# Feed-forward input products of a split-fp32 block stack: three products of 256 columns, or one of 512 and one of 256

## What is computed

```
def rms_norm(x, g):
    y = x * rsqrt(mean(x * x, axis=-1) + 1e-6)
    return y * g

def swiglu(x, w_in, w_out):            # w_in 1024 x 5632, w_out 2816 x 1024
    g, u = split(x @ w_in, 2)
    return (silu(g) * u) @ w_out

for i in range(2):
    h = h + 0.5 * swiglu(rms_norm(h, ffn1_norm[i]), ffn1_w_in[i], ffn1_w_out[i])
    h = h + mixer_i(rms_norm(h, mix_norm[i]))      # recurrent, then spatial gating
    h = h + 0.5 * swiglu(rms_norm(h, ffn2_norm[i]), ffn2_w_in[i], ffn2_w_out[i])
```

## Time and profile before

| | |
|---|---|
| median of 3 runs | 1516.98 us (1516.81 to 1517.42) |
| profiled execution, its time | 1516.46 us |
| its span | 1514.7 us |
| TensorE products in flight | 1473.3 us, 97% |
| VectorE busy | 1051.7 us, 69% |
| ScalarE busy | 770.3 us, 51% |
| GpSimd busy | 293.9 us, 19% |
| DMA | 239.15 MB, mean 158 GB/s |

### The profile page before, as it was taken

The page is one execution under the profiler, slowest core; times in us unless marked ns, Lnnn a source line. Parts: engine busy times, 40 slices in busy tenths (PEclk is TensorE's granted clock), DMA queues, the critical chain, the costliest instruction groups (busy, mean ns, idle before and its releaser), DMA issues.

```text
span 1514.7 us, 31434 instructions
## 1 busy us (share of the span) xinstructions
PE 1473.3 (97%) x11919; PEld 1454.8 (96%) x11919; DVE 1051.7 (69%) x2005; ACT 770.3 (51%) x1296; POOL 293.9 (19%) x361
## 2 busy tenths in 40 slices
PE   7999999899999999999999999999999999999998
PEld 7999999899999999999999999999999999999898
DVE  6666578766655666557766665898768769976883
ACT  5455448554544545445454544536744453575442
POOL 4111113211102111024221113422240125121000
PEclk9999999999999999999999999999999999999999
DMA  6666754465555556555465555543343554434333
GB/s 203 186 186 201 222 171 132 149 192 180 183 177 184 183 181 191 172 192 168 140 194 174 186 163 172 167 112 108 97 115 101 167 141 140 116 95 125 112 119 119
DMA packets 245276, 239.15 MB, mean 158 GB/s; under 512 B 15160, under 2 KB 244392, under 8 KB 245176
## 3 DMA queue, kind: packets, MB, share of 16 engines
q1 hardware_dynamic: 245176, 237.78, 51.5%
HBM read 236.70 MB, written 1.05 MB: 157 GB/s over the span
## 4 chain that ended last, share of the span: by engine, by line
PE 84%; DVE 11%; ACT 2%; issue 2%; POOL 1%; DMA 0%; SPq 0%; DVEq 0%; ACTq 0%; POOLq 0%
PE bank L565 25%; PE bank L567 25%; PE bank L566 25%; DVE w_lo L1561 3%; DVE work L2023 1%; PE bank L893 1%; PE bank L851 1%; PE bank L833 1%; DVE work L1711 1%; PE bank L762 1%; PE bank L816 1%; PE bank L899 1%; PE bank L909 1%; DVE work L1594 1%; PE bank L832 0%
## 5 line engine op out<-in xcount | busy, mean ns | idle before, releaser
L1561 DVE TENSOR_TENSOR w_lo<-raw,w_hi 128x1024 fp32r<-128x1024 f32 (+1 forms) x456 | 558.3, 1234 | 296.5 <-ACT w_hi L982 296.1
L565 PE MATMUL bank<-x_hi,w_hi 128*128 128x256 f32 (+1 forms) x2480 | 717.1, 289 | 1.7 <-DVE w_lo L1561 1.6
L567 PE MATMUL bank<-x_hi,w_lo 128*128 128x256 f32 (+1 forms) x2480 | 705.7, 285 | 0.0
L566 PE MATMUL bank<-x_lo,w_hi 128*128 128x256 f32 (+1 forms) x2480 | 705.0, 284 | 0.0
L982 ACT CAST w_hi<-raw 128x1024 fp32r<-128x1024 f32 (+1 forms) x456 | 464.4, 1028 | 237.4 <-PE bank L567 227.1
L565 PEld LDWEIGHTS bank<-x_hi,w_hi 128*128 128x128 f32 x2480 | 474.3, 191 | 3.5 <-issue 2.0
L566 PEld LDWEIGHTS bank<-x_lo,w_hi 128*128 128x128 f32 x2480 | 474.4, 191 | 0.9
L567 PEld LDWEIGHTS bank<-x_hi,w_lo 128*128 128x128 f32 x2480 | 474.1, 191 | 0.0
L565 PE MATMUL bank<-y_hi,w_hi 128*128 128x256 f32 (+1 forms) x1088 | 310.6, 285 | 8.3 <-DVE y_lo L1572 8.3
L567 PE MATMUL bank<-y_hi,w_lo 128*128 128x256 f32 (+1 forms) x1088 | 309.7, 285 | 0.0
L566 PE MATMUL bank<-y_lo,w_hi 128*128 128x256 f32 (+1 forms) x1088 | 309.6, 285 | 0.0
(11 more groups left out here) (296 smaller groups left out, 1204.1 us busy)
## 6 DMA issues: line engine op xcount, KB each, us to landing
raw<-in_ffn_w_in_dram SPq DMA_DIRECT2D x176, 512.0 KB, 3.6
raw<-in_w_in_dram SPq DMA_DIRECT2D x100, 512.0 KB, 3.6
raw<-in_ffn_w_out_dram SPq DMA_DIRECT2D x64, 512.0 KB, 4.3
raw<-in_w_out_dram SPq DMA_DIRECT2D x32, 512.0 KB, 3.5
raw<-in_ffn_w_out_dram SPq DMA_DIRECT2D x32, 384.0 KB, 3.1
raw<-in_rec_w_in_dram SPq DMA_DIRECT2D x16, 512.0 KB, 3.5
raw<-in_sg_w_in_dram SPq DMA_DIRECT2D x16, 512.0 KB, 3.6
raw<-in_rec_w_out_dram SPq DMA_DIRECT2D x8, 512.0 KB, 3.5
```

What stands on the lines that cost most here:

```text
L565: mm(acc, wh, xh, start=first and j == 0, stop=False)
L566: mm(acc, wh, xl, start=False, stop=False)
L567: i_ = mm(acc, wl, xh, start=False, stop=last and j == n - 1)
L1561: TT(w_lo[:, s, 0:n, :], raw[:, s, 0:n, :], w_hi[:, s, 0:n, :].bitcast(fp32), SUB).then_inc(lo_made, 1)
```

## The change

x_hi and x_lo become the two halves of one tensor x_both, y_hi and y_lo those of y_both. In the in stages (both=True) a k takes two products: upper weights with both halves of the activations, 512 columns, a whole bank (columns 0 to 255 upper, 256 to 511 lower), and lower weights with the upper activations, into columns 256 to 511. A tile is then the sum of its bank's two halves. ScalarE copies the second half to SBUF (low_half, into ffn_b, which lies in the tensor pre, not in use there), VectorE adds the first half out of the bank, and multiplies the sum in SBUF; this second operation marks the bank as read. All other stages have three products of one k as before.

```diff
         w_hi = sb("w_hi", [P, RING, KU, CU], fp32r)
...
-        x_hi = sb("x_hi", [P, NC8 * L], fp32r)
-        x_lo = sb("x_lo", [P, NC8 * L], fp32r)
...
+        x_both = sb("x_both", [P, 2, NC8 * L], fp32r)
+        y_both = sb("y_both", [P, 2, NF * SEQ], fp32r)
+        x_hi, x_lo = x_both[:, 0, :], x_both[:, 1, :]
+        y_hi, y_lo = y_both[:, 0, :], y_both[:, 1, :]
...
+        ffn_b = pre[:, :, 3:3 + SEQ]
...
+                        if both:
+                            mm(bank[T % 4][:, 0:2 * N], wh, xs[:, :, a:b], start=first and j == 0, stop=False)
+                            i_ = mm(bank[T % 4][:, N:2 * N], wl, xs[:, 0, a:b], start=False, stop=last and j == n - 1)
                         else:
...
-                        mm(acc, wh, xh, start=first and j == 0, stop=False)
-                        mm(acc, wh, xl, start=False, stop=False)
-                        i_ = mm(acc, wl, xh, start=False, stop=last and j == n - 1)
+                            mm(acc, wh, xs[:, 0, a:b], start=first and j == 0, stop=False)
+                            mm(acc, wh, xs[:, 1, a:b], start=False, stop=False)
+                            i_ = mm(acc, wl, xs[:, 0, a:b], start=False, stop=last and j == n - 1)
...
+            def low_half(pr, m, i):
+
+                if m == 0:
+                    act.wait_ge(first_done, FIRSTS[pr] + 1 + 2 * i)
+                else:
+                    act.wait_ge(unit_done, units_of(pr)[-1][0] + 1 + 4 * i)
+                nc.scalar.copy(ffn_b[:, m, :], bank[(2 * pr + m) % 4][:, SEQ:2 * SEQ]).then_inc(low_copied, 1)
+
             def gate_turn(pb, ub, i, first=None):
...
                 for m in range(2):
+                    low_half(pb, m, i)
+                for m in range(2):
                     act.wait_ge(tile_read, 2 * pb + m + 1 + o4)
                     activation(ffn_s[:, m, :], ffn_t[:, m, :], ACT.Silu).then_inc(silu_done, 1)
                 for U in (ub + 2, ub + 3):
                     split_w(U + LEAD, o)
+                for m in range(2):
+                    low_half(pb + 1, m, i)
...
                 for m in range(2):
-                    scaled(pb, m, ffn_t[:, m, :], SEQ, META, o)
+                    dve.wait_ge(low_copied, 44 * f + m + 1 + 4 * i)
+                    TT(ffn_t[:, m, :], tile(pb, m, SEQ), ffn_b[:, m, :], ADD).then_inc(halves_added, 1)
+                for m in range(2):
+                    dve.wait_ge(halves_added, 44 * f + m + 1 + 4 * i)
+                    TT(ffn_t[:, m, :], ffn_t[:, m, :], rstd[:, META:L], MUL).then_inc(tile_read, 1)
                 for U in (ub + 2, ub + 3):
                     split_w(U + LEAD, o)
                 for m in range(2):
-                    wait_tile(pb + 1, m, o)
+                    dve.wait_ge(low_copied, 44 * f + m + 3 + 4 * i)
+                    TT(ffn_h[:, m, :], tile(pb + 1, m, SEQ), ffn_b[:, m, :], ADD).then_inc(halves_added, 1)
+                for m in range(2):
+                    dve.wait_ge(halves_added, 44 * f + m + 3 + 4 * i)
                     dve.wait_ge(gate_scaled, 22 * f + m + 1 + 2 * i)
-                    TT(ffn_h[:, m, :], tile(pb + 1, m, SEQ), ffn_r[:, m, :], MUL).then_inc(tile_read, 1)
+                    TT(ffn_h[:, m, :], ffn_h[:, m, :], ffn_r[:, m, :], MUL).then_inc(tile_read, 1)
```

More of the change, by code:

```diff
@@ L206, in build_stack @@
         h = sb("h", [P, NC8, L])
-        x_hi = sb("x_hi", [P, NC8 * L], fp32r)
-        x_lo = sb("x_lo", [P, NC8 * L], fp32r)
-        y_hi = sb("y_hi", [P, NF * SEQ], fp32r)
-        y_lo = sb("y_lo", [P, NF * SEQ], fp32r)
+        x_both = sb("x_both", [P, 2, NC8 * L], fp32r)
+        y_both = sb("y_both", [P, 2, NF * SEQ], fp32r)
+        x_hi, x_lo = x_both[:, 0, :], x_both[:, 1, :]
+        y_hi, y_lo = y_both[:, 0, :], y_both[:, 1, :]
         con = sb("con", [P, CONST_ALL])
@@ L322, in build_stack @@
         act_new = sem("act_new")
-        silu_done, gate_scaled = sem("silu_done"), sem("gate_scaled")
+        silu_done, gate_scaled, low_copied, halves_added = (
+            sem(n) for n in ("silu_done", "gate_scaled", "low_copied", "halves_added"))
         meta_loaded, meta_t, meta_read, padded = (sem(n) for n in ("meta_loaded", "meta_t", "meta_read", "padded"))
@@ L544, in unit @@
             def unit(U, k0, n, pair, npair_off, xs, N, first, last, ready, off, tiles=2, wide_x=False,
-                     mid=None):
-                hi, lo = xs
+                     mid=None, both=False):
                 pe.wait_ge(lo_made, U + 1 + off)
@@ L560, in unit @@
                         wh, wl = (t[:, s, j, m * P:(m + 1) * P] for t in (w_hi, w_lo))
-                        if N == SEQ and wide_x:
-                            xh, xl = (t[:, k * L + META:(k + 1) * L] for t in (hi, lo))
-                        else:
-                            xh, xl = xview(hi, k, N), xview(lo, k, N)
-                        mm(acc, wh, xh, start=first and j == 0, stop=False)
-                        mm(acc, wh, xl, start=False, stop=False)
-                        i_ = mm(acc, wl, xh, start=False, stop=last and j == n - 1)
+                        a, b = (k * L + META, (k + 1) * L) if N == SEQ and wide_x else (k * N, (k + 1) * N)
+                        if both:
+                            mm(bank[T % 4][:, 0:2 * N], wh, xs[:, :, a:b], start=first and j == 0, stop=False)
+                            i_ = mm(bank[T % 4][:, N:2 * N], wl, xs[:, 0, a:b], start=False, stop=last and j == n - 1)
+                        else:
+                            mm(acc, wh, xs[:, 0, a:b], start=first and j == 0, stop=False)
+                            mm(acc, wh, xs[:, 1, a:b], start=False, stop=False)
+                            i_ = mm(acc, wl, xs[:, 0, a:b], start=False, stop=last and j == n - 1)
                     if last and m == 0 and tiles == 2:
@@ L577, in _, with pair @@
             off_half = [0]
-            def pair(pr, xs, N, ready=None, after=None, tiles=2, wide_x=False, mid=None):
+            def pair(pr, xs, N, ready=None, after=None, tiles=2, wide_x=False, mid=None, both=False):
                 us = units_of(pr)
                 for j, (U, k0, n) in enumerate(us):
-                    unit(U, k0, n, pr, 0, xs, N, j == 0, j == len(us) - 1, ready, 0, tiles, wide_x, mid)
+                    unit(U, k0, n, pr, 0, xs, N, j == 0, j == len(us) - 1, ready, 0, tiles, wide_x, mid, both)
                     if after is not None:
                         after(j)
-            xs, ys = (x_hi, x_lo), (y_hi, y_lo)
+            xs, ys = x_both, y_both
             def norm_sum(n, T0):
@@ L602, in in_phase @@
                     pair(pb + p, xs, SEQ, ready=ready if p == 0 else None,
-                         after=(lambda j: norm_sum(n, META) if j == 1 else None) if p == 0 else None)
+                         after=(lambda j: norm_sum(n, META) if j == 1 else None) if p == 0 else None, both=True)
                 if name == "in01":
@@ L610, in in_phase @@
                         for j, (U, k0, nk) in enumerate(us):
-                            unit(U, k0, nk, pb + p, 0, xs, SEQ, j == 0, j == 1, None, 4 * i)
+                            unit(U, k0, nk, pb + p, 0, xs, SEQ, j == 0, j == 1, None, 4 * i, both=True)
             def out_phase(name, ready, N=SEQ, after=None):
```

## The result

The changed kernel takes 1505.74 us (median of 4, 1504.62 to 1509.10) beside 1517.20 for the kernel before. The ratio is 0.9929, with a 95% interval of 0.9915 to 0.9943. The gain is 11.5 us; forecast were 18.5. The time lies in the range, 7 us above the forecast. The profile is of the slowest of the four executions, 1509.10 us.

A forecast was written before the change was run, and what follows sets the result against it. The prediction took TensorE's stream of products as the bound. Products saving 18.7 us and 0.2 us charged at the first stage's end made 1516.98 - 18.5 = 1498.4 us; range 1482 to 1507, held at 0.80.

The forecast's parts named there:

- What bounds the kernel: Whole kernel: TensorE's stream of products binds, in flight 97% of the span; VectorE and ScalarE matter only where TensorE waits.
- rival C: Four in stages: products as forecast, but ScalarE and VectorE bind a little, half turn 5.8 us; 1501 to 1507, chance 0.11.
- The saving per group: Four in stages: a group goes from 360.0 to 346.7 ns, 13.3 less on 1408 groups, 18.7 us.
- I take 226.7: Four in stages: a 512-column product costs 226.7 ns, its columns' 213.3 plus 13.3 per product; bounds 216 and 240.
- Rival B: Four in stages: the wide product hides the extra, 216 to 219 ns; 1482 to 1489 us, chance 0.27.
- The straight line through 256 and 272 columns: TensorE's fp32r product times, 6.2 ns for 16 columns, carried on to 512 columns: 219 ns, so the extra may shrink.
- the fp32 records: TensorE's fp32 products at L833 and L851: 215 to 217.5 ns per 512-cycle record, an extra of only 2 to 4 ns.
- the rule that the prediction took for a warm product: TensorE: N/2.4 + 2.5 ns; gain 3.7 us for all products, 34 for the wide alone; not in the sum.
- Rival D: Four in stages: extra goes with columns, or the half-to-half jump costs a product, 237 to 240 ns; 1513 to 1517, chance 0.10.
- Copies and additions: Four in stages: four 0.4 us ScalarE copies and four 0.42 us VectorE additions a turn, hidden; w_lo 3.8 us early.
- E: Rival, chance 0.10: in the four in stages the chain of ScalarE and VectorE binds; 24 us slower, 1541 us.
- The end of in01: End of the first stage: the 1.2 us longer tail leaves no slack before out01's weights; 0.2 us charged, bounds 0 and 1.

The follow-up runs named there:

- alternating order: The changed kernel with the decays behind out01's first weight split and, in every second k, the narrow product ahead of the wide one; 1500.53 us, ratio 0.9898.

## Why the prediction was right, and where it was off

**What bounds the kernel** was right: all of the gain is in TensorE's stream, and with three products and all of the new work beside them the kernel stands at 1.0007 of before.

**The time** lies in the stated range, but not in the forecast's own part of it, 1496 to 1501: it lies where rival C stood, whose cause did not occur. That the range held is in part luck.

**The saving per group** is the term that was mis-sized. Forecast were 13.3 ns on all 1408 groups, 18.7 us. In01's loop has it (13.5), the other groups have half (6.7): 11.6 us in the profiled execution. The step that failed is "I take 226.7", with a price that belongs to each product and is the same everywhere; of the 11.1 us by which the profiled execution falls short of the forecast's gain (18.5 - 7.4), it makes 7.1 (18.7 - 11.6), and out01 3.25 (3.45 - 0.2). In place of one value the runs showed two, 346.7 and 353.3 ns a group, which last until the stream is interrupted; the rows of before could not show it, since there a group of three is at 360 in all stages. Nor is the price equal for wide and narrow: wide behind wide is 231 ns, 18 over its columns, and in in01's loop the wide one costs 231.6 and the narrow one 115.0 in the mean (one pair: rows at 59.77 and 60.00). Their sum is the forecast's 346.7, its parts, 226.7 and 120.0, are not: that this stage came out right is two errors that cancel. In the slower stream they are 236.7 and 116.7.

**Rival B**, a wide product of 216 ns, is refuted: no mean was under 230, and no single distance that is given here under 224. The straight line through 256 and 272 columns was no guide, and neither were the fp32 records with their small extra. So is, for this stream, the rule that the prediction took for a warm product, 215.8 ns for 512 columns, from the Trainium skill, "TensorE: Matmul & The Clock Gate", section "Back-to-back issue gap", which gives it as the isolated gap of a single product. 231 is what the run shows. **Rival D**, no gain, is refuted by its time; its point that the extra may partly go with the columns is supported by the wide product's 18 ns.

**Copies and additions** were right to the tenth: 0.38 us a copy (0.4 forecast), 0.42 an addition, a half turn of 5.3 us without TensorE, no wait in a turn, w_lo 3.6 to 3.9 us ahead where 3.8 were forecast. So rivals C and E are refuted as mechanisms, though the measured time lies in C's range.

**The end of in01** was seen as the tight place and priced too low: 0.2 us with bounds 0 and 1, against 1.7 us of waiting, and with the half clock 3.45 us. What I left out was the transfer. ScalarE's cast of out01's first weights already waited for their landing in the kernel before, 1.96 us:

```profile
137.44 1.05 ACT L982 CAST w_hi<-raw 128x1024 fp32r<-128x1024 f32 x1 [1.96 <-DMA raw<-in_ffn_w_out_dram]
```

In the changed kernel this cast starts 1.65 us earlier (135.79), but TensorE's first product of out01 3.9 us earlier (140.89 against 144.82). The forecast counted only the longer tail, 0.36 us when measured by itself with in01 as long as before. Where in01's loop is at 353.3 ns, and the stage 2.2 us longer than in the changed kernel, TensorE waits 0.8 us; in the others with neither cure 1.4 to 1.7. The two experiments that take away the late landing or the decays show that with either gone the rest fits.

## What to carry to other kernels

Fewer and wider products pay when the distance between two starts is longer than their columns; read the distance from the first and the last start of many, in each stage by itself, since one program can show two speeds and a mean hides it. Before such a change is counted, look at what the shorter stage will meet earlier: the transfer that was just in time and the chain that was just short enough. And when runs of a kernel spread more after a change than before, compare single stages between profiles, those that the change doesn't touch too, before believing a difference of 2 us.

## What the runs showed of the hardware that I had not expected

A stream of fp32r products that take turns at 512 and 256 columns, each with its own weights, at full clock, runs at 346.7 or at 353.3 ns a pair. It kept its value for 320 pairs (113 us), through a loop's branches and while the other engines and the transfers went on, and can change it when a few other products come between: two transposes ahead of the loop took in01, in11 and in12 from 353.3 to 346.5, and left in02 at 353.3. The slower value is a pattern of three pairs that repeats. Six pairs ahead of in01's sums ran at 353 in one execution and at 346 in another of the same program. Streams of 256 columns alone (120.0 ns) had one value only. The alternating order had one value, 348.3. What the line-up is of (weights, activations, or the writing into the bank) stays open: no run here looked inside it, and I have no way yet to force the faster value save by the order of the products.
